# Five input pairs of a two-block layer with three sum steps each in place of two, two thirds of their first sums made by an accumulating transfer

## The reference

```python
h = rms_norm(x, norm_g)
proj = jnp.einsum('bsd,dn->bsn', h, w_in)          # 2048 -> 19,536 columns
(q_a, k_a, v_a, o_a, i_a, f_a, z_a, c_q, c_kv, k_r, z_b, g_a, g_b) = jnp.split(proj, offsets, axis=-1)
...
h_a = rms_norm(h_a, ...)                            # mLSTM over 8 heads, from q_a, k_a, v_a, i_a, f_a
y_a = jnp.einsum('bsc,cd->bsd', jax.nn.sigmoid(o_a) * h_a * jax.nn.silu(z_a), w_a)
...
y = jax.nn.sigmoid(g_a) * y_a + jax.nn.sigmoid(g_b) * y_b
return x + jnp.einsum('bsd,de->bse', y, w_out)      # then a second block with an MLP of 8192
```

## Time and profile before

| | |
|---|---|
| three runs | 2097.47, 2097.56, 2098.32 us |
| the profiled execution, by its own clock on the device | 2098.16 us, span 2096.4 us |
| granted TensorE clock | 0.999 of full speed |
| PE busy | 2081.1 us, 99% of the span |
| DVE busy, ACT busy | 1452.1 us (69%), 1120.2 us (53%) |
| pairs 0 to 6 | from 152.6 us to about 450 us |

### The profile page before, as it was taken

How to read it: one execution, slowest core, us unless ns; L and a number is a source line. 1 busy time by engine, 2 the same in 40 slices (tenths; PEclk the granted TensorE clock), 3 DMA queues, 4 the chain that set the end, 5 groups by cost and what they waited for, 6 DMA issues and landing times.

```text
span 2096.4 us, 25089 instructions
## 1 busy us (share of the span) xinstructions
PE 2081.1 (99%) x10024; PEld 1746.8 (83%) x10024; DVE 1452.1 (69%) x1893; ACT 1120.2 (53%) x1466; POOL 69.5 (3%) x85
## 2 busy tenths in 40 slices
PE   9999999999999999999999999999999999999998
PEld 7888888888888888888888888888888888888886
DVE  6877888875555786556554455466996896797694
ACT  6555555555444675554454454354664565465463
POOL 0000000000000020000000000000010000000000
PEclk9999999999999999999999999999999999999999
DMA  8556455564465544465755542455476477577563
GB/s 334 183 179 206 175 208 214 186 249 176 175 228 201 186 145 161 141 224 198 299 186 185 189 161 101 162 200 184 179 243 228 161 243 234 178 223 247 191 208 128
DMA packets 62196, 413.88 MB, mean 197 GB/s; under 512 B 7040, under 2 KB 7680, under 8 KB 14720
## 3 DMA queue, kind: packets, MB, share of 16 engines
q1 hardware_dynamic: 53856, 382.71, 51.2%
q0 software_dynamic: 7648, 28.84, 4.9%
q10 hardware_dynamic: 576, 0.73, 0.1%
HBM read 394.69 MB, written 8.39 MB: 192 GB/s over the span
## 4 chain that ended last, share of the span: by engine, by line
PE 94%; DVE 2%; DMA 2%; ACT 1%; issue 1%; SPq 0%; POOL 0%; POOLq 0%; DVEq 0%; ACTq 0%
PE proj L659 15%; PE proj L661 15%; PE proj L660 15%; PE proj L1118 11%; PE proj L1122 6%; PE proj L758 4%; PE proj L760 4%; PE proj L759 4%; PE tbank L758 2%; PE tbank L759 2%; PE tbank L760 2%; PE tbank L614 2%; PE bank_a L758 1%; PE bank_a L760 1%; PE bank_a L759 1%; DMA nat<-stg 1%
## 5 line engine op out<-in xcount | busy, mean ns | idle before, releaser
L1827 DVE TENSOR_TENSOR w_lo<-raw,w_hi 128x1024 fp32r<-128x1024 f32 (+1 forms) x627 | 740.2, 1195 | 503.6 <-ACT w_hi L1227 496.7
L1227 ACT ACTIVATE w_hi<-raw 128x1024 fp32r<-128x1024 f32 (+1 forms) x627 | 641.7, 1035 | 707.4 <-PE proj L661 462.6
L659 PE MATMUL proj<-w_hi,a_both 128*128 128x512 f32 x1280 | 512.3, 400 | 1.3 <-DVE w_lo L1827 0.8
L661 PE MATMUL proj<-w_hi,a_both 128*128 128x512 f32 x1280 | 499.9, 391 | 0.0
L660 PE MATMUL proj<-w_lo,a_both 128*128 128x512 f32 x1280 | 498.4, 389 | 0.0
L661 PEld LDWEIGHTS proj<-w_hi,a_both 128*128 128x128 f32 x1280 | 240.2, 188 | 51.8
L659 PEld LDWEIGHTS proj<-w_hi,a_both 128*128 128x128 f32 x1280 | 240.5, 188 | 49.3 <-DVE a_both L1914 1.3
L660 PEld LDWEIGHTS proj<-w_lo,a_both 128*128 128x128 f32 x1280 | 240.7, 188 | 47.5
L1118 PE MATMUL proj<-a_both,w_hi 128*128 128x512 f32 x672 | 160.6, 391 | 0.3 <-DVE a_both L1873 0.3
L1118 PEld LDWEIGHTS proj<-a_both,w_hi 128*128 128x128 f32 x672 | 123.5, 188 | 24.4 <-DVE a_both L1873 0.5
L1827 DVE TENSOR_TENSOR w_lo_deep<-raw,w_hi_deep 128x1024 fp32r<-128x1024 f32 x86 | 98.3, 1164 | 49.1 <-ACT w_hi_deep L1227 49.0
(11 more groups left out here) (530 smaller groups left out, 3086.5 us busy)
## 6 DMA issues: line engine op xcount, KB each, us to landing
raw<-stream SPq DMA_DIRECT2D x358, 1024.0 KB, 4.8
nat<-stg POOLq DMA_DIRECT2D x35, 256.0 KB, 8.7
nat<-x SPq DMA_DIRECT2D x2, 1024.0 KB, 16.7
z_store<-z POOLq DMA_DIRECT2D x1, 2048.0 KB, 8.6
ga_store<-z POOLq DMA_DIRECT2D x1, 2048.0 KB, 12.4
gb_store<-z POOLq DMA_DIRECT2D x4, 512.0 KB, 6.9
yb<-z_store POOLq DMA_DIRECT2D x4, 512.0 KB, 9.4
ga<-ga_store POOLq DMA_DIRECT2D x1, 2048.0 KB, 8.6
```

Of the source, the lines that this page charges most:

```text
L659: nc.tensor.matmul(banks[t][:, :], ah, wh, start=first, stop=False)
L661: last = nc.tensor.matmul(banks[t][:, :], al, wh, start=False, stop=end)
L1227: A(hi_places[s][:, 0:width], src, ACT.Copy).then_inc(w_rounded, 1)
L1827: V.tensor_tensor(lo_places[s][:, 0:width], src, hi_places[s][:, 0:width].bitcast(f32), SUB).then_inc(w_rest, 1)
```

## The change

Pairs 0 to 4 get sum steps at 1, 3 and 5, with a third set of activation sums (rows of group 6, `xs_hi_3`, `xs_lo_3`), made in the last slots of the second projection of v_a ahead of pair 0. The last two pairs stay as they are. Of these fifteen weight sums the first and second of each pair get their first instruction (the 1024 wide one) from two transfers: SP copies the unit's last block twice into `w_sum_vo`, and POOL adds the first and third block onto it, straight from HBM. The last block is then left out of the unit's own load. DVE waits for the added sums in place of making them, and does the two 512 wide sums as before. `rope_k` moves by one step in pair 0. At the start ACT splits three pieces between the two sums of squares and two behind them, DVE accordingly.

```diff
-GROUPS_IN = (1, 4)
-SUM_AT_IN = [(2, 5)] + [(3, 5)] * 4 + [(2, 5)] * 2
-ORDER_IN = [(0, 2, 1, 3, 5, 4, 6, 7) if at[0] == 2 else (0, 2, 3, 1, 5, 4, 6, 7) for at in SUM_AT_IN]
+GROUPS_IN = (1, 4, 6)
+SUM_AT_IN = [(1, 3, 5)] * 5 + [(2, 5)] * 2
+ORDER_IN = [(0, 2, 1, 3, 5, 4, 6, 7) if len(at) == 2 else (0, 1, 2, 4, 3, 6, 5, 7) for at in SUM_AT_IN]
...
+BY_DMA = [i for i in range(SUMS_VO) if i % 3 < 2]
...
+            def copy_last_block(i):
+
+                if i < 2:
+                    sp.wait_ge(small_t, 1)
+                    sp.wait_ge(sumsq, 2)
+                else:
+                    sp.wait_ge(w_rest, FIRST_PIECE[SUM_UNITS[i - 2]] + 4)
+                both = w_sums(i)[:, 0:PIECE].rearrange("p (b c) -> p b c", b=2)
+                last_block = stream[SUM_UNITS[i]][:, 3 * CW:4 * CW].unsqueeze(1).to_broadcast([P, 2, CW])
+                sp.dma_start(both, last_block).then_inc(w_copied[i % 2], 16)
+
             for u in range(RING, UNITS):
                 sp.wait_ge(w_rest, FIRST_PIECE[u - RING] + 2)
-                sp.dma_start(raw[:, u % RING, :], stream[u]).then_inc(raw_landed[u % RING], 16)
+                width = 3 * CW if u in copies else 4 * CW
+                sp.dma_start(raw[:, u % RING, 0:width], stream[u][:, 0:width]).then_inc(raw_landed[u % RING], 16)
+                if u + 2 in copies:
+                    copy_last_block(copies[u + 2])
...
+            for i in BY_DMA:
+                pool.wait_ge(w_copied[i % 2], 16 * (1 + sum(n < i and n % 2 == i % 2 for n in BY_DMA)))
+                both = w_sums(i)[:, 0:PIECE].rearrange("p (b c) -> p b c", b=2)
+                first_and_third = stream[SUM_UNITS[i]].rearrange("p (b c) -> p b c", b=4)[:, 0:3:2, :]
+                pool.dma_start(both, first_and_third, accum_op=ADD).then_inc(w_added[i % 2], 16)
...
             square_sum(scr[:, :], nat[:, 0, :], ss1[:, 0:1])
-            split()
+            split(3)
             act.wait_ge(x_ready[1], 16)
             square_sum(scr[:, :], nat[:, 1, :], ss1[:, 1:2])
-            split(RING)
+            split(RING - 2)
...
-                V.tensor_tensor(s[:, 0:2, :], b[:, 0:3:2, :], b[:, 3, :].unsqueeze(1).to_broadcast([P, 2, CW]),
-                                ADD).then_inc(w_summed, 1)
-                dve.wait_ge(w_summed, 2 * i + 1)
+                if i in BY_DMA:
+                    dve.wait_ge(w_added[i % 2], 16 * (1 + sum(n < i and n % 2 == i % 2 for n in BY_DMA)))
+                    dve.sem_inc(w_summed, 1)
+                else:
+                    V.tensor_tensor(s[:, 0:2, :], b[:, 0:3:2, :], b[:, 3, :].unsqueeze(1).to_broadcast([P, 2, CW]),
+                                    ADD).then_inc(w_summed, 1)
+                    dve.wait_ge(w_summed, 2 * i + 1)
...
-                        if p == 0 and step == 3 and j == 0:
+                        if p == 0 and step == 4 and j == 0:
                             rope_k()
...
+                if i == 1 and j == 5:
+                    sum_x(2)
+                if i == 1 and j == 7:
+                    rest_of_x_sums(2)
```

More of the change, by code:

```diff
@@ L51 @@
 SUM_UNITS = _sum_units()
-SUMS_IN = 2 * PAIRS_IN
+SUMS_IN = sum(len(at) for at in SUM_AT_IN)
+SUMS_VO = sum(len(at) for at in SUM_AT_IN[:5])
+BY_DMA = [i for i in range(SUMS_VO) if i % 3 < 2]
 def _pieces():
@@ L204, in build @@
         xs_lo = place("xs_lo", [P, 2, 4, P], f32r, 148.25)
+        xs_hi_3 = place("xs_hi_3", [P, 4, P], f32r, 176.25)
+        xs_lo_3 = place("xs_lo_3", [P, 4, P], f32r, 178.25)
+        xs_his = [xs_hi[:, 0], xs_hi[:, 1], xs_hi_3]
+        xs_los = [xs_lo[:, 0], xs_lo[:, 1], xs_lo_3]
         joined = place("joined", [P, 4, CW], f32, 152.25)
@@ L341, in w_sums @@
         def w_sums(i):
-            if i < 2 * 5:
+            if i < SUMS_VO:
                 return w_sum_vo[:, i % 2, :]
@@ L445, in build @@
         w_summed = sem("w_summed")
+        w_copied = [sem(f"w_copied{i}") for i in range(2)]
+        w_added = [sem(f"w_added{i}") for i in range(2)]
         ms_summed = sem("ms_summed")
@@ L494, in _ @@
             sp.dma_start(nat[:, 0, :], x_v[:, 0, :]).then_inc(x_ready[0], 16)
+            copies = {SUM_UNITS[i]: i for i in BY_DMA}
+            def copy_last_block(i):
[7 more added lines that the diff above has]
+                sp.dma_start(both, last_block).then_inc(w_copied[i % 2], 16)
             for u in range(RING, UNITS):
                 sp.wait_ge(w_rest, FIRST_PIECE[u - RING] + 2)
-                sp.dma_start(raw[:, u % RING, :], stream[u]).then_inc(raw_landed[u % RING], 16)
+                width = 3 * CW if u in copies else 4 * CW
+                sp.dma_start(raw[:, u % RING, 0:width], stream[u][:, 0:width]).then_inc(raw_landed[u % RING], 16)
+                if u + 2 in copies:
+                    copy_last_block(copies[u + 2])
                 if u == RING:
@@ L830, in pair_in @@
                         i = at.index(step)
-                        sum_step(kt, whole, mixed, a_hi, a_lo, xs_hi[:, i], xs_lo[:, i], i + 1, i == 0, i == len(at) - 1)
+                        sum_step(kt, whole, mixed, a_hi, a_lo, xs_his[i], xs_los[i], i + 1, i == 0, i == len(at) - 1)
                     elif step == STEPS - 1:
@@ L1347, in round_x_sums @@
                 act.wait_ge(ms_summed, i + 1)
-                A(xs_hi[:, i, :, :], xs[:, :, :], ACT.Copy).then_inc(ms_rounded, 1)
+                A(xs_his[i][:, :, :], xs[:, :, :], ACT.Copy).then_inc(ms_rounded, 1)
             def k_slot(j, i):
@@ L1421, in _, with v_slot @@
             for i in range(2):
-                pieces(slot=(lambda j: (conv_slot(j), exp_slot(j))) if i == 0 else lambda j: exp_slot(8 + j))
+                def v_slot(j):
+                    if i == 0:
+                        conv_slot(j)
+                    elif j == 6:
+                        round_x_sums(2)
+                    exp_slot(8 * i + j)
+                pieces(slot=v_slot)
                 for t, b in enumerate(banks()):
@@ L2065, in rest_of_x_sums @@
                 dve.wait_ge(ms_rounded, i + 1)
-                V.tensor_tensor(xs_lo[:, i, :, :], xs[:, :, :], xs_hi[:, i, :, :].bitcast(f32), SUB).then_inc(ms_rest, 1)
+                V.tensor_tensor(xs_los[i][:, :, :], xs[:, :, :], xs_his[i][:, :, :].bitcast(f32), SUB).then_inc(ms_rest, 1)
             def k_slot(j, i):
```

## The result

| | before | after |
|---|---|---|
| median, and all runs | 2097.43 us (2096.46 to 2098.32, 9 runs) | 2103.43 us (2101.85 to 2106.52, 9 runs) |
| ratio to before | | 1.0029, 95% interval 1.002 to 1.0038 |
| the profiled execution, its span | 2098.16, 2096.4 us | 2103.45, 2101.6 us |

The changed kernel is 6.0 us slower; the forecast was 4.0 slower, 2101.6, and the measured time is inside its range. The interval of the ratio begins at the 0.2% that a measurement can tell.

A forecast was written before the change was run, and what follows sets the result against it. PE, busy 99% of the span, was taken as the bound. The terms -3.4 - 1.1 + 7.1 + 0.3 + 0.8 + 0.3 made +4.0 us, forecast 2101.6 us, with an 8 in 10 range of 2100.0 to 2107.5.

The forecast's parts named there:

- The gating: Pairs 2 to 4: gating behind step 1's fourth piece delays step 2's piece, a 2.25 us gap each; +7.1 us in all.
- Rival 2: Not slower: the gap at step 2 does not open, 2093.4 to 2094.5 us; chance 0.08.
- Fewer products: Five more sum steps on PE, one product less in each; -3.4 us.
- The start: PE's gap near 31 us closes with three pieces ahead of the second sum of squares; -1.1 us.
- Pair 1: No gating there, but two copies on ACT make the piece of step 2 late; +0.3 us.
- Pair 0: Sines and their table load on ACT make the piece of step 2 late; +0.8 us.
- The sum step at 3 in pair 0: Pair 0 gets the other pairs' gap between the pieces of step 4, from DVE's sums for step 5; +0.3 us.
- (1): DVE's two short sums ahead of the join before a pair, 1.33 us, just covered; 0 to 0.1 us a pair.
- (2): Third activation sums on DVE, some 3 us, put at no cost; uncovered 1 to 3 us once.
- (4): SP's copy waits only for pieces the load behind it waits for anyway, so no load is later; no cost.
- (5): POOL has nothing else in its queue when it issues the adds; no cost.
- Rival 1: Added sums for step 1 land after their 18.0 us lead, delaying the join in four pairs; 2109 to 2120 us, chance 0.22.

The follow-up runs named there:

- e1: Changed kernel with DVE's gating in pairs 2 to 4 moved from step 1's last piece to behind the third piece of steps 3 and 5; 2095.70 us.
- e5: Changed kernel with SP's copies for step 1 of pairs 1 to 4 issued one unit later; 2143.73 us.
- e9: Changed kernel with gating and ACT's work later, sigmoid table loaded early, DVE's sums behind the second piece of the plain step; 2091.64 us.
- e10: Kernel before (two sum steps) with the new start and DVE's sums behind the second piece of the plain step; 2094.17 us.
- e3: Kernel before with only the new order of the start, three pieces between the two sums of squares; 2095.90 us.
- e4: Changed kernel with all fifteen weight sums made by DVE and no adding transfer; 2112.55 us.
- e7: Changed kernel with a one-column sigmoid on ACT in pair 1, which loads the table early; 2102.91 us.
- e8: Changed kernel with ACT's sigmoids, copies and sines behind the pieces of step 2, DVE's gating left in place; 2117.73 us.

## Why the prediction was right, and where it fell short

The direction and the mechanism are right, and the 2101.6 is 1.8 under the median. The median also lies above 2102.8, the upper bound that the forecast's own terms allow. That it is within the range is in part luck: the room up to 2107.5 was there for late adds, which did not come.

**The gating, +7.1, is what happened, at its place and size.** In pair 3 PE's wait is 2.25 us, the forecast's number to the hundredth, and the first matmul behind it takes 0.11 where 0.1 was put. e1 moves this one item and the gaps of pairs 3 and 4 are gone. Rival 2 is refuted: the gap stands in all three pairs.

**Mis-sized was the same term in pair 2.** It was worked out in pair 3 and multiplied by three. The sum holds neither the 1.28 us of the table load nor the clock behind a gap. Pair 2 is 2.34 us longer than pair 3: 0.64 of gap, 1.5 of the clock (the starts behind the gap take 1.6 more than 0.23 each, those in pair 3 take 0.1), and 0.2 for two starts 0.34 apart in step 1 (from 244.97 on), which pair 2 of e1 has as well and whose cause is open. The table load was to be had from the trace of before, in the same slot of pair 2; that it would cost there what it did was not looked at.

```profile
241.43 1.28 ACT L1382 ACT_TABLE_LOAD   x1
```

The fall of the clock was not in the trace of before at this place, which has no gap of that length here. With the two, 4.0 becomes 6.3, beside the 6.0 measured.

**The clock also makes the spread.** The nine runs of the changed kernel lie in three heaps, 2101.85 to 2102.21 with a mean granted clock of 0.999, 2103.43 to 2103.76 with 0.998, and one at 2106.52 with 0.996, and e1's eleven runs in one, 1.2 us wide. Four of the nine runs lie 0.25 to 0.6 over the forecast, and by their mean clock they had no such stretch. Read so, 2101.6 was about the time of an execution whose clock held; that it can hold behind pair 2's gap is seen in e5. That the heaps are stretches at the lower level was seen in the one profiled execution of the middle heap; for the others it is argued from their mean clock.

**Fewer products, -3.4:** e9 against e10 gives -2.5 - 0.5 = -3.0 for it. In their traces pairs 1 to 4 are 41.5 us long against 42.16, 0.63 less a pair, which makes 3.1 of five. **The start, -1.1:** 1.35 in the trace and 1.3 in e3. **Pair 1, +0.3:** 0.33 of gap and 0.11, 0.44. **Pair 0, +0.8:** 0.53 and 0.11, 0.64. **The sum step at 3 in pair 0, +0.3:** 0.34, at 174.89.

**At nothing.** (1) The two short sums ahead of the join were covered: no pair begins with a gap. e4, with 1.22 us more at that place, has one of 0.85 in each of four pairs. (2), (4) and (5): from 100 to 152 us, where the activation sums are made, PE waits for nothing, and from 100 to 375 DVE waits for ACT's `w_hi` (45.6 us, 38 times), once 0.2 us for an instruction of its own, and for no load or transfer. (3) `rope_k` cost nothing in the changed kernel; it made the gap of 0.4 in e9, where the sums come later.

**Rival 1, 0.22, did not come,** and its lead was right. For pair 2 SP issued the copy at 212.75 and POOL the add at 217.93; it landed at 227.9, and DVE's first sum stands at 230.69, so nobody waited. In pairs 1 to 4 copy and add together took 15.6, 15.2, 15.1 and 16.4 us where 16 to 17 were put, the adds of them 9.7 to 11.4 where 11 to 12 were put: 1.6 us were left in pair 4, 2.6 to 2.9 in the others. The medians of all ten, 5.7 and 8.8, are no measure of this, since the adds for step 3 are the shorter ones (7.4 to 8.0 in these pairs) and have the longer lead. e5 shows the rest of the rival: once the lead is spent, every microsecond is a gap (DVE waits 8.78, 6.89, 7.57 and 7.56 us, and PE stands 0.33 less each time).

The Trainium skill, DMA: Bandwidth & Descriptors, in its section on the anatomy of one DMA (SWDGE path), has a fit that makes 3.2 us of a 512 KB transfer from that queue. The adding transfers here took 8.8 (5.8 to 11.4), and the measured numbers decide. The prediction used the fit for SP's copy as well, which is not from that queue; the 6.4 us that it made of the two were 15.1 to 16.4. The rival did not come, but not by that margin.

The Trainium skill, ScalarE: Activation LUTs, in its section on what ACT_TABLE_LOAD costs, gives about 1.28 us for the load and 1.38 for a drain, 2.66 together. Here the load starts 0.02 behind the end of the rounding ahead of it, takes 1.28, and the sigmoid starts 1.30 behind the load's start: this trace shows the load and no drain, and 0.64 of it in the gap.

**Still open** is when a gap lowers the clock, below. Also not separated: about 0.08 us a pair, by which the pairs are longer than their steps and gaps add up to (44.26 against 41.48 + 2.36 + 0.34 in pair 3).

## What to carry to other kernels

A ring that is counted in pieces is not a fixed lead in time: turn a step from two long pieces into four short ones, and everything that is scheduled "four pieces ahead" moves twice as near to its deadline (here 10.9 us of PE became 4.76). For each side job on the producers, work out which piece is now the first behind it and when that piece is wanted; the whole loss here was one such place, and moving it (with the table load and the sums) turned 6.0 us of loss into 5.3 of gain. Work the case out for each repetition, the first one above all, which carries costs that come once, such as a table load.

## What the runs showed of the hardware

A gap costs more than its idle time. Behind each gap of 0.2 us and more, where the clock holds, the next matmul starts 0.33 to 0.34 behind the first in place of 0.23. Behind longer ones TensorE's clock can fall to its lower level for a few matmuls, which then start 0.42 to 0.43 apart. The last column counts the matmuls behind a gap whose next one starts 0.40 us or more later:

| gap, us of idle | kernel, place | matmuls at the lower level behind it |
|---|---|---|
| 0.2 to 0.9 | all kernels | none |
| 2.25 | changed kernel, pairs 3 and 4 | none |
| 2.26 | e7, pair 2; pairs 3 and 4 | 7; none |
| 2.26 | e4, pair 3; pair 4 | 7; none |
| 2.25 | e5, pair 3; pair 4 | 7; none |
| 2.9 | changed kernel, pair 2; e4, pair 2; e5, pair 2 | 7; 7; none |
| 5.3 to 6.7 | e8, pairs 2 to 4 | 13, 8, 13 |
| 6.6 to 8.5 | e5, pairs 1 to 4 | 8, 9, 9, 8 |

Every gap of 5.3 us or more was followed by such a stretch. Of nine gaps of about 2.25 us three were, and of three of 2.9 two, so such a gap costs either its own length or about 1.5 us more (7 matmuls, 0.2 each), and the times spread by that. What decides it in these cases was not found.

An adding transfer's duration depends on what else is under way. Of the ten adds of 512 KB in the changed kernel those for step 1 of pairs 1 to 4 took 9.7 to 11.4 us and those for step 3 7.4 to 8.0. In e5, where the two of a pair overlapped, they took 11.0 to 13.2 and 9.4 to 11.5, and the copies for step 1 7.6 to 8.0 where they had taken 4.6 to 5.6. A lead that is worked out from durations in one order of the transfers can be too short in another.
